# A fused hybrid layer on one core: one scan, one load, the gate's matmuls and one residual are moved in their queues

## The chip, the cores and the metric

The kernel runs on one core of a Trainium2 chip. Its time is the device time of one execution in microseconds (us). The median of three runs of the kernel before is 702.98 us (702.5 to 704.5).

## The reference

One transformer-like layer in float32 for 512 tokens of width 1024:

- The input is normalised and projected to an S5 branch `u` (512 channels) and to q, k, v of 8 heads of 64.
- S5 branch: a diagonal complex state space in 32 groups, then `y = gelu(C s + d_skip * u)` and the gate `y * sigmoid(y @ w_glu + b_glu)`, with `w_glu` 512x512.
- Attention branch: block attention with a relative bias and a softmax per head.
- Both branches are normalised, joined and multiplied with `w_out`, and added to the input.
- Cross attention of 4 heads of 128 over 256 memory rows follows (`x_wq`, `x_wkv`, `x_wo`), and is added.
- A feed-forward block follows: `w_up` (1024 to 5632), a causal convolution of width 3, `silu(gate) * val`, `w_down`, and is added.

## The kernel before

All five engines run programs written out by hand in Bass, one block for each engine, and every engine takes its instructions in the order written. Semaphores link them. Helpers: `filled`/`read` say that TensorE has filled a PSUM bank and that somebody may read it, `drained`/`fill` say that a bank has been read and may be filled again. `plan()` lists for each of the eight banks which result follows which. So a matmul group can wait for the reader of the result that stood in the same bank before.

**Matmuls in three passes.** Each float32 product is taken as hi*hi + hi*lo + lo*hi (`mm3`, L515 to L517). Weights come in "units" of 128x1024 numbers, two to a "chunk" of 1 MB. `load_chunk` (L461 to L468) waits until the two units that stood in its half of the raw buffer have been split, `hi_done` and `lo_done`, and then issues the transfer. For chunk c it waits for 2(c-1) high parts and as many low parts. `split_hi` (ScalarE, L487) makes the high part in a ring of four units, `split_lo` (VectorE, L498) the low part, and TensorE waits for `lo_done`. Some chunks are loaded from SyncE's queue and chunks 4 to 10 from ScalarE's own program, where the wait of `load_chunk` stands in front of all that ScalarE has behind it.

**S5 stages.** The state space goes in four quarters q. For each, TensorE makes `w1r`, `w1i`, the kernels `ka`, `kb` and the states `vr`, `vi`. VectorE's `scan(q)` reads the states in PSUM and writes `zb`. ScalarE copies the kernels into `kt`, and SyncE's `t_load(q)` (L618) spreads them into the Toeplitz matrix `toep` by eight small DMAs. `outputs(q, ...)` on TensorE needs `toep` and the scan. The result goes out and back through DRAM (`y_write`, `y_back`), VectorE adds the skip (`skip_in`), ScalarE takes `gelu(q)`, and GpSimd splits it for the gate (`glu_input`, `glu_in`). Between these TensorE works on the q, k, v and memory projections. After the fifth of eight q/k units, TensorE transposes q in four parts, `qt0` to `qt3`, which go to banks 6, 7, 6, 7, and ScalarE's `qt_evac` empties them. The transposes stand between the four tiles of unit 10.

**The attention loop** has 32 steps s (4 token tiles x 8 heads). TensorE works at even s: in steps 0 to 6 two tiles of the memory's v (`mv_tile`), in the steps of `GLU_AT` the gate's matmuls (`glu_half`, six matmuls of 512 columns each; gate m goes to result `zm`), then the products with v of the step before (`values`), the scores of the next two heads (`scores`), and the transposes of two probability tiles (`pt`). ScalarE takes at odd s the copy of a `pt` and the exponentials of two heads, then what the tables say: `split_hi` of a unit (`SPLIT_AT`), the gate's tanh, `gelu(3)` (an activation table of its own, so that a table is loaded before it and again before the next exponential), `mem_rows("mv", ...)`, which empties `mv0` at s = 7 and `mv1` at s = 9. VectorE takes `logits` of two heads (the bias and the maximum), the copy of a `pt`, `skip_in(3)` at s = 4, the rows of the memory's k at s = 5, and `split_lo` one step behind `split_hi`. The banks say: `mv0` then `z1` in bank 2, `mv1` then `z2` in bank 0, `mk1`, `z0`, `z3` in bank 1.

**Before the feed-forward block** VectorE works in this order: `xo_lo(3)`, `x3_mean(1)`, `x3_rows(1)` (it waits for a power taken on GpSimd), `w_residual(2)` for both halves of 512 columns, `x_lo("x3", 0)`, `split_lo(U_UP)`, `x_lo("x3", 1)`. The last is what the first matmul of `up_half` waits for.

Of the kernel before, what the change touches and what calls it, by code (L numbers as in the profile page):

```python
# [59 lines left out]

GLU_AT = [8, 10, 12, 14]
SS_AT, MK_ROWS_AT = 19, 2

SOUT_AT = [(16, 0, 0), (16, 0, 1), (18, 1, 0), (20, 0, 2), (20, 0, 3), (22, 1, 2), (22, 1, 1), (24, 1, 3), (24, 2, 0),
# [2 lines left out]

XO_AT = [5, 6, 7, 8]  # L70

SPLIT_AT = {0: 22, 1: 23, 2: 24, 4: 25, 9: 26, 11: 27, 13: 28, 16: 29, 29: 30, 31: 31}
YA_AT = [20, 22, 27]


# [25 lines left out]
def layer(nc, A, out):  # L101
# [10 lines left out]
    with ctx:  # L112
# [255 lines left out]
        def after_drain(eng, name, r=0):  # L368

            bank, n = uses[name]  # L370
            eng.wait_ge(bank_free[bank], r + (n + 1))
# [89 lines left out]
        def load_chunk(eng, c, r=0):  # L461
            if c >= 2:

                eng.wait_ge(hi_done, r * 4 + 2 * (c - 1))
                eng.wait_ge(lo_done, r * 4 + 2 * (c - 1))
            src = chunk_src(c, r)
            eng.dma_start(raw[:, c % 2, :].rearrange("p (k n) -> p k n", k=src.shape[1]), src)\
               .then_inc(raw_in[c % 2], 16)  # L468
# [424 lines left out]
        def _(act):  # L893
# [67 lines left out]
            c = COL["attn_qn"]  # L961
# [51 lines left out]
            def kt_evac(t):  # L1013
                c = COL["attn_kn"]
                drained(A_(kT[:, :, t * 128:(t + 1) * 128], read(act, f"kt{t}")[:, :].rearrange("p (a b) -> p a b", a=4),
                           ACT.Copy, scale=gcol[:, c:c + 1]), f"kt{t}")

            def gelu(q):
                act.wait_ge(zz_ready, q + 1)
                A_(to_tokens(yT[:, q, :]), uT[:, q, :].rearrange("p (i k) -> p i k", i=L), ACT.Gelu_apprx_tanh)\  # L1020
                    .then_inc(gelu_ready, 1)
# [48 lines left out]
                kt_evac(t - 1)  # L1070
            split_hi(act, 19)
            kt_evac(TT - 1)
            load_chunk(act, 10)
            split_hi(act, 20)
            for q in range(3):
                gelu(q)
            split_hi(act, 21)

            def mem_rows(name, dst, t):
# [43 lines left out]
            for s in range(TT * H):  # L1123
                if s % 2 == 1:
                    pt_evac(act, lambda o, i: A_(o, i, ACT.Copy), s - 1)
                if s % 2 == 1 and s + 1 < TT * H:
                    probabilities(s + 1)
                    if s > H and s % H == 1:
                        factors_in(s // H - 1)
                    probabilities(s + 2)  # L1130
                if s in GLU_AT:
                    m = GLU_AT.index(s)

                    if m == 0:
                        act.wait_ge(hb_ready, 1)
                    drained(A_(sg[:, m, :], read(act, f"z{m}")[:, :], ACT.Tanh, scale=0.5, bias=hbglu[:, m:m + 1]), f"z{m}")
                if s - 2 in GLU_AT:
                    c = GLU_AT.index(s - 2)
                    act.wait_ge(y2_ready, c + 1)
                    g = COL["gnorm_ssm"] + c  # L1140
                    A_(xs[:, 0, c, :], yT[:, c, :], ACT.Copy, scale=gcol[:, g:g + 1]).then_inc(act_hi, 1)
                    A_(sg[:, c, :], yT[:, c, :], ACT.Square).then_inc(ysq_ready, 1)
                if s in SPLIT_AT:
                    split_hi(act, SPLIT_AT[s])
                if s == 4:
                    gelu(3)
                if s in (7, 9):
                    mem_rows("mv", xv, s // 9)
                if s in YA_AT:
                    ya_square(YA_AT.index(s))  # L1150
                if s - 1 in YA_AT:
                    ya_hi(YA_AT.index(s - 1))
# [122 lines left out]
        def _(dve):  # L1275
# [62 lines left out]
            def head_rows(name, src, tiles, heads, width):  # L1338
                root(name)
                for t in tiles:  # L1340
                    c = EVC[name] + (t - tiles[0]) * heads
                    v = src[:, t, :].rearrange("p (h n) -> p h n", h=heads)
                    tt(v, v, rs[:, c:c + heads].unsqueeze(2).to_broadcast([128, heads, width]), ALU.mult)\
                        .then_inc(xn_ready, 1)
# [172 lines left out]
            head_event("q", qk, range(TT), H, "q")  # L1517
            split_lo(dve, 10)
            head_rows("q", qk, range(TT), H, HD)
            after_drain(dve, "par")  # L1520
            b = COL["ssm_b_glu"]
            V.tensor_scalar_mul(hbglu[:, :], gcol[:, b:b + 4], 0.5).then_inc(hb_ready, 1)
            split_lo(dve, 11)
            root("mem", mem_ready)
            scan(1)
            split_lo(dve, 12)
            split_lo(dve, 13)
            skip_in(0)
            head_event("k", qk, (0, 1), H, "k", False)
# [67 lines left out]
            for s in range(TT * H):  # L1597
                if s % 2 == 1 and s + 1 < TT * H:
                    logits(s + 1)
                    logits(s + 2)  # L1600
                if s % 2 == 1 and s + 1 < TT * H:
                    p = pt_evac(dve, V.tensor_copy, s)
                if s >= H and s % H == 0:
                    inverse_sums(s // H - 1)
                if s == SS_AT:
                    drained(V.tensor_copy(ev(sq, "ss"), p[:, 384:384 + TT]), f"pt{SS_AT}")
                    after_drain(dve, f"pt{SS_AT}")
                    mean_sq("ss")
                    root("ss")
                    dve.wait_ge(h_in, 16 * TT)  # L1610
                if s > H and s % H == 2:
                    ya_scale(s // H - 1)
                if s == 4:
                    skip_in(3)
                if s in (MK_ROWS_AT, MK_ROWS_AT + 1):
                    t = s - MK_ROWS_AT
                    head_event("mk", mkrow, [t], XH, "mk", t == MT - 1)
                if s == MK_ROWS_AT + 3:
                    head_rows("mk", mkrow, range(MT), XH, XD)
                if s - 3 in GLU_AT:  # L1620
                    cc = GLU_AT.index(s - 3)
                    g = gcol[:, COL["gnorm_ssm"] + cc:COL["gnorm_ssm"] + cc + 1]
                    lo_of(yT[:, cc, :], xs[:, 0, cc, :], xs[:, 1, cc, :], g).then_inc(ym_ready, 1)
                if s - 1 in YA_AT:
                    ya_lo(YA_AT.index(s - 1))
                if s - 1 in GLU_AT:
                    m = GLU_AT.index(s - 1)
                    after_drain(dve, f"z{m}")
                    stt(yT[:, m, :], sg[:, m, :], 1.0, yT[:, m, :], ALU.add, ALU.mult).then_inc(y2_ready, 1)
                for n, at in enumerate(G_ADD_AT):  # L1630
                    if at == s:
                        g_residual(n)
                if s - 1 in SPLIT_AT and SPLIT_AT[s - 1] != U_OUT + 3:
                    split_lo(dve, SPLIT_AT[s - 1])
                if s == 2 * H + 2:
                    split_lo(dve, U_OUT + 3)
# [44 lines left out]
            def xo_lo(t):  # L1681
                v = [bs[:, i, :].rearrange("p (a n) -> p a n", a=4)[:, :, t * 128:(t + 1) * 128] for i in range(2)]
                tile_lo(f"xo{t}", v[0], v[1])
# [53 lines left out]
            x3_rows(0)  # L1737
            w_residual(1, [1])
            xo_lo(TT - 1)
            x3_mean(1)  # L1740
            x3_rows(1)
            w_residual(2)
            x_lo("x3", 0)
            dve.wait_ge(lo_done, U_UP)
            split_lo(dve, U_UP)
# [56 lines left out]
        def _(pe):  # L1802
# [383 lines left out]
            for s in range(0, TT * H, 2):  # L2186
                if s < H:
                    mv_tile(s)
                    mv_tile(s + 1)
                if s in GLU_AT:  # L2190
                    for half in range(2):
                        pe.wait_ge(glu_in, 2 + 2 * half)
                        glu_half(GLU_AT.index(s), half)
                for at, t, i in SOUT_AT:
                    if at == s:
                        sout_piece(t, i)
                if s >= 2:
                    values(s - 2)
                if s + 2 < TT * H:
                    scores(s + 2)  # L2200
                prob_transposes("pt", "sc", s, s // H + 1, 4)
                prob_transposes("pt", "sc", s + 1, s // H + 1, 4, s + 1 != SS_AT)
                if s >= H and s % H == 0:
                    factors(s // H - 1)
                if s + 1 == SS_AT:

                    pe.wait_ge(ones_ok, 1)
                    pe.wait_ge(ysum_ready, 1)
                    p = pb[uses[f"pt{SS_AT}"][0]]
                    for t in range(TT):  # L2210
                        last = mm(p[:, 384 + t:385 + t], sg[:, 0, t * 128:(t + 1) * 128], ones[:, 0:1])
                    filled(last, f"pt{SS_AT}")
# [191 lines left out]
```

## Time and profile before

| | |
|---|---|
| median of 3 runs | 702.98 us (702.5 to 704.5) |
| the profiled execution | 705.13 us |
| its span, first to last instruction | 703.5 us |
| TensorE busy | 687.4 us (98%) |
| VectorE, ScalarE, GpSimd busy | 415.0, 320.2, 142.4 us |
| mean granted TensorE clock | 0.998 |

The span is what the trace covers; 1.6 us of the profiled execution's time lie around it. TensorE is busy in all but some 16 us, so the time can only fall where TensorE stands idle, and it rises with every new idle time there. Times in rows are us from the start of the span unless marked ns. PE is TensorE, DVE VectorE, ACT ScalarE, POOL GpSimd, SP SyncE; a q behind the name is the sequencer, which issues DMAs.

### The profile page before, as it was taken

How to read it: one execution, taken by the hardware profiler on the slowest of the kernel's cores; microseconds unless marked ns; L12 is line 12 of the kernel's file. 1: busy time of each engine (PE TensorE's matmuls, PEld its weight loads, DVE VectorE, ACT ScalarE, POOL GpSimd, SP SyncE). 2: the span in 40 equal slices, each digit the busy share in tenths (PEclk: the TensorE clock that was granted, in tenths of full speed). 3: DMA queues.
4: the chain of work that ended last, by engine and by line, in shares of the span. 5: the costliest groups of instructions: out<-in, count | busy, mean ns of one | idle time of the engine just before them, and what ended most of it. 6: DMA issues, size and time to landing. Idle time of an engine off the chain costs nothing.

```text
span 703.5 us, 11258 instructions
## 1 busy us (share of the span) xinstructions
PE 687.4 (98%) x4105; PEld 566.0 (80%) x4105; DVE 415.0 (59%) x697; ACT 320.2 (46%) x559; POOL 142.4 (20%) x139
## 2 busy tenths in 40 slices
PE   8999999988999999999999999999999999999998
PEld 8977767866777788888898888888888888888886
DVE  4999977737765657556865555555455563333333
ACT  5738453656854635664454333333343433222320
POOL 4999994032031111240100000000000000000000
PEclk9999999999999999999999999999999999999999
DMA  8648445258210123030313313223233133132203
GB/s 255 220 136 131 144 106 152 60 184 290 99 61 1 55 96 121 1 119 1 121 62 119 119 60 119 97 82 119 63 116 116 63 119 114 66 119 77 102 0 120
DMA packets 63000, 73.97 MB, mean 105 GB/s; under 512 B 20873, under 2 KB 47796, under 8 KB 62836
## 3 DMA queue, kind: packets, MB, share of 16 engines
q1 hardware_dynamic: 59172, 66.12, 29.8%
q10 hardware_dynamic: 3792, 7.36, 3.2%
q8 instruction: 24, 0.39, 0.3%
q14 instruction: 12, 0.10, 0.0%
HBM read 68.08 MB, written 5.78 MB: 105 GB/s over the span
## 4 chain that ended last, share of the span: by engine, by line
PE 76%; DVE 11%; DMA 4%; ACT 4%; issue 3%; SPq 2%; ACTq 0%; POOL 0%; DVEq 0%
PE pb L515 22%; PE pb L517 22%; PE pb L516 22%; PE pb L1804 6%; DVE F L1286 4%; PE pb L1807 4%; DVE wring L498 2%; ACT F L902 1%; DMA raw<-in_w_in 1%; DMA raw<-in_ssm_w_glu 1%; DMA raw<-in_x_wkv 1%; DMA scr_y<-F 1%; SPq L618 1%; DVE F L1292 1%; DVE pb L1286 1%
## 5 line engine op out<-in xcount | busy, mean ns | idle before, releaser
L515 PE MATMUL pb<-xs,wring 128*128 128x512 f32 (+1 forms) x448 | 165.3, 369 | 1.0 <-DVE xs L1292 1.0
L498 DVE TENSOR_TENSOR wring<-raw,wring 128x1024 fp32r<-128x1024 f32 x95 | 124.1, 1309 | 69.0 <-ACT wring L487 68.8
L517 PE MATMUL pb<-xs,wring 128*128 128x512 f32 (+1 forms) x448 | 164.3, 367 | 0.0
L516 PE MATMUL pb<-xs,wring 128*128 128x512 f32 (+1 forms) x448 | 164.3, 367 | 0.0
L487 ACT ACTIVATE wring<-raw 128x1024 fp32r<-128x1024 f32 x100 | 105.1, 1054 | 89.2 <-PE pb L517 70.1
L1292 DVE SCALAR_TENSOR_TENSOR F<-pb,ccol,F 128x511 f32<-128x511 f32 x88 | 66.0, 750 | 103.4 <-ACT F L902 97.5
L515 PE MATMUL pb<-wring,bs 128*128 128x512 f32 x240 | 96.7, 403 | 0.1
L515 PEld LDWEIGHTS pb<-xs,wring 128*128 128x128 f32 x448 | 84.5, 189 | 15.3 <-issue 1.4
L517 PEld LDWEIGHTS pb<-xs,wring 128*128 128x128 f32 x448 | 84.5, 189 | 13.6
L516 PEld LDWEIGHTS pb<-xs,wring 128*128 128x128 f32 x448 | 84.6, 189 | 13.6
L517 PE MATMUL pb<-wring,bs 128*128 128x512 f32 x240 | 94.1, 392 | 0.0
L516 PE MATMUL pb<-wring,bs 128*128 128x512 f32 x240 | 94.0, 392 | 0.0
L902 ACT ACTIVATE F<-pb,ccol 128x512 f32<-128x512 f32 x44 | 34.2, 778 | 121.4 <-PE pb L517 117.5
L515 PE MATMUL pb<-wring,xs 128*128 128x512 f32 x192 | 81.1, 422 | 0.5 <-DVE wring L501 0.3
L517 PE MATMUL pb<-wring,xs 128*128 128x512 f32 x192 | 75.4, 393 | 0.0
L516 PE MATMUL pb<-wring,xs 128*128 128x512 f32 x192 | 75.1, 391 | 0.0
L1804 PE MATMUL pb<-F 128*64 128x64 f32 (+6 forms) x1056 | 63.3, 261 | 6.9 <-DMA F<-F 2.1
L1804 PEld LDWEIGHTS pb<-F 128*64 128x64 f32 (+4 forms) x1056 | 47.5, 144 | 24.7 <-issue 16.1
L902 ACT ACTIVATE F<-pb 16x128 f32<-16x128 f32 (+5 forms) x84 | 31.1, 383 | 56.0 <-PE pb L1807 44.6
L515 PEld LDWEIGHTS pb<-wring,bs 128*128 128x128 f32 x240 | 45.4, 189 | 9.9 <-POOL wring L869 0.3
L517 PEld LDWEIGHTS pb<-wring,bs 128*128 128x128 f32 x240 | 45.4, 189 | 9.7
L516 PEld LDWEIGHTS pb<-wring,bs 128*128 128x128 f32 x240 | 45.5, 189 | 8.8
(147 smaller groups left out, 790.3 us busy)
## 6 DMA issues: line engine op xcount, KB each, us to landing
raw<-in_ffn_w_up SPq DMA_DIRECT2D x22, 1024.0 KB, 5.1
raw<-in_ffn_w_down SPq DMA_DIRECT2D x11, 1024.0 KB, 4.8
F<-in_x SPq DMA_DIRECT2D x8, 512.0 KB, 5.9
raw<-in_w_in ACTq DMA_DIRECT2D x4, 1024.0 KB, 5.6
raw<-in_w_out SPq DMA_DIRECT2D x4, 1024.0 KB, 4.8
raw<-in_w_in SPq DMA_DIRECT2D x3, 1024.0 KB, 6.3
raw<-in_x_wkv ACTq DMA_DIRECT2D x3, 1024.0 KB, 6.0
raw<-in_x_wq SPq DMA_DIRECT2D x2, 1024.0 KB, 5.4
```

Source lines behind the costliest of these rows:

```text
L487: ins = nc.scalar.activation(w_unit(u, 0), raw_unit(u), ACT.Copy)
L498: ins = nc.vector.tensor_tensor(w_unit(u, 1), raw_unit(u), w_unit(u, 0).bitcast(f32), ALU.subtract)
L515: nc.tensor.matmul(ps, lh, rh, start=first, stop=False)
L516: nc.tensor.matmul(ps, lh, rl_, start=False, stop=False)
L517: return nc.tensor.matmul(ps, ll, rh, start=False, stop=last)
L618: sync.dma_start(toep[d * CG:(d + 1) * CG, :, (L - 1 - d) * CG:], kt[0:CG, :, 0:(d + 1) * CG]).then_inc(t_in[q], 16)
L902: return nc.scalar.activation(o, i, f, **k)
L1286: return V.tensor_tensor(o, a, b, op)
L1292: return V.scalar_tensor_tensor(out=o, in0=a, scalar=s1, in1=b, op0=o1, op1=o2)
L1804: return nc.tensor.matmul(o, l, r, start=start, stop=stop)
L1807: return nc.tensor.transpose(o, i, ident[0:i.shape[0], 0:i.shape[0]])
```

## The change

The change moves work in the queues and adds or removes none:

1. VectorE: `scan(1)` comes straight after the q rows, ahead of `split_lo(11)`, the gate's bias, `split_lo(12)` and the memory's root.
2. ScalarE: `gelu(0)` and `gelu(1)` stand ahead of `load_chunk(act, 10)` and `split_hi(act, 20)`; `gelu(2)` stays behind them.
3. Attention loop: the gate's four tiles no longer take two halves each at s = 8, 10, 12, 14. The first halves of gates 0 and 1 stand at s = 8, their second halves at s = 10. The tanh of the four is at s = 10, 11, 12, 14, and what follows it on ScalarE and VectorE moves with it.
4. `split_hi(24)` moves from s = 2 to s = 3 (and its `split_lo` from 3 to 4), `gelu(3)` from s = 4 to s = 5, where it stands behind the exponentials of that step.
5. VectorE: `w_residual(2)` is cut: the first half goes ahead of `x3_mean(1)`, the second ahead of `x3_rows(1)`.

```
-GLU_AT = [8, 10, 12, 14]
+GLU_AT = {8: [(0, 0), (1, 0)], 10: [(0, 1), (1, 1)], 12: [(2, 0), (2, 1)], 14: [(3, 0), (3, 1)]}
+TANH_AT = [10, 11, 12, 14]
-SPLIT_AT = {0: 22, 1: 23, 2: 24, 4: 25, 9: 26, 11: 27, 13: 28, 16: 29, 29: 30, 31: 31}
+SPLIT_AT = {0: 22, 1: 23, 3: 24, 4: 25, 9: 26, 11: 27, 13: 28, 16: 29, 29: 30, 31: 31}
@@ ScalarE
             kt_evac(TT - 1)
+            gelu(0)
+            gelu(1)
             load_chunk(act, 10)
             split_hi(act, 20)
-            for q in range(3):
-                gelu(q)
+            gelu(2)
             split_hi(act, 21)
...
-                if s in GLU_AT:
-                    m = GLU_AT.index(s)
+                if s in TANH_AT:
+                    m = TANH_AT.index(s)
...
-                if s - 2 in GLU_AT:
-                    c = GLU_AT.index(s - 2)
+                if s - 2 in TANH_AT:
+                    c = TANH_AT.index(s - 2)
...
-                if s == 4:
+                if s == 5:
                     gelu(3)
@@ VectorE
             head_rows("q", qk, range(TT), H, HD)
+            scan(1)
+            split_lo(dve, 11)
             after_drain(dve, "par")
             b = COL["ssm_b_glu"]
             V.tensor_scalar_mul(hbglu[:, :], gcol[:, b:b + 4], 0.5).then_inc(hb_ready, 1)
-            split_lo(dve, 11)
+            split_lo(dve, 12)
             root("mem", mem_ready)
-            scan(1)
-            split_lo(dve, 12)
             split_lo(dve, 13)
...
-                if s - 3 in GLU_AT:
-                    cc = GLU_AT.index(s - 3)
+                if s - 3 in TANH_AT:
+                    cc = TANH_AT.index(s - 3)
...
-                if s - 1 in GLU_AT:
-                    m = GLU_AT.index(s - 1)
+                if s - 1 in TANH_AT:
+                    m = TANH_AT.index(s - 1)
...
             xo_lo(TT - 1)
+            w_residual(2, [0])
             x3_mean(1)
+            w_residual(2, [1])
             x3_rows(1)
-            w_residual(2)
             x_lo("x3", 0)
@@ TensorE
-                if s in GLU_AT:
-                    for half in range(2):
-                        pe.wait_ge(glu_in, 2 + 2 * half)
-                        glu_half(GLU_AT.index(s), half)
+                for m, half in GLU_AT.get(s, []):
+                    pe.wait_ge(glu_in, 2 + 2 * half)
+                    glu_half(m, half)
```

## Rows read from the trace of the kernel before

**Rows 1.** Waits of TensorE: engine, tile, line <- releaser: total us, times, longest.
```profile
PE pb L1804 <- ACT pbuf L902: 2.1, 2, 1.7
...
PE pb L1804 <- ACT F L902: 0.7, 1, 0.7
```

**Rows 2.** Timeline of TensorE, 81 to 92: start, duration, what, [idle before <- releaser].
```profile
85.06 0.60 PE L1807 MATMUL pb<-ident,F 128*128 128x128 f32 x4
...
90.38 0.84 PE L1804 MATMUL pb<-F 128*64 128x64 f32 x24 [1.51 <-DVE F L1286]
```

**Rows 3.** Timeline of VectorE, 77 to 91.
```profile
77.04 1.55 DVE L1286 TENSOR_TENSOR F<-F,rs 128x512 f32<-128x512 f32 x1
...
79.46 1.22 DVE L498 TENSOR_TENSOR wring<-raw,wring 128x1024 fp32r<-128x1024 f32 x1
...
84.14 0.42 DVE L1286 TENSOR_TENSOR pb<-pb,F 128x256 f32<-128x256 f32 x1
...
90.09 1.68 DVE L498 TENSOR_TENSOR wring<-raw,wring 128x1024 fp32r<-128x1024 f32 x1
```

**Rows 4.** Timeline of ScalarE and its sequencer, 76 to 89.
```profile
80.76 0.37 ACTq L467 DMA_DIRECT2D raw<-in_w_in  x1
82.09 0.69 ACT L902 ACTIVATE F<-pb,gq 128x512 f32<-128x512 f32 x1 [4.19 <-PE pb L1807]
```

**Rows 5.** Timeline of GpSimd, 75 to 92.
```profile
84.28 1.42 POOL L810 TENSOR_TENSOR F<-F 128x576 f32<-128x576 f32 x1
```

**Rows 6.** Timeline of ScalarE, 103.5 to 107, around the load of chunk 8.
```profile
104.84 0.38 ACTq L467 DMA_DIRECT2D raw<-in_x_wkv  x1
105.05 0.83 ACT L902 ACTIVATE F<-pb 16x128 f32<-16x128 f32 x3
```

**Rows 7.** Timeline of ScalarE, 135.8 to 145, around the load of chunk 10.
```profile
137.02 0.69 ACT L902 ACTIVATE F<-pb,gcol 128x512 f32<-128x512 f32 x1
137.08 0.39 ACTq L467 DMA_DIRECT2D raw<-in_x_wkv  x1
143.43 1.06 ACT L487 ACTIVATE wring<-raw 128x1024 fp32r<-128x1024 f32 x1 [5.72 <-DMA raw<-in_x_wkv]
```

**Rows 8.** Timeline of SyncE, 131 to 159: the eight DMAs of `t_load(3)`.
```profile
131.92 6.18 SPq L618 DMA_DIRECT2D F<-F  x8
```

**Rows 9.** Timeline of TensorE at four later places.
```profile
143.63 1.11 PE L1804 MATMUL pb<-F 128*64 128x64 f32 x24 [2.12 <-DMA F<-F]
...
171.99 0.71 PE L1804 MATMUL pb<-F 64*128 64x128 f32 x8 [1.73 <-ACT pbuf L902]
...
172.83 0.48 PE L515 MATMUL pb<-xs,wring 128*128 128x512 f32 x1
...
337.89 0.36 PE L515 MATMUL pb<-xs,wring 128*128 128x256 f32 x1 [1.00 <-DVE xs L1292]
```

**Rows 10.** Windows: stretch: us, busy by engine, then granted clock, DMA share, GB/s.
```profile
143.90:147.30 3.40, 3.40 (x29) 2.38 (x24) 0.00 (x0) 3.37 (x4) 0.22 (x1) 0.50 0.21 48
...
170.30:172.00 1.70, 0.01 (x2) 0.04 (x2) 1.12 (x1) 1.53 (x5) 1.62 (x2) 1.00 0.74 277
```

**Rows 11.** Timeline of ScalarE, 163 to 175.
```profile
164.19 1.06 ACT L487 ACTIVATE wring<-raw 128x1024 fp32r<-128x1024 f32 x1 [3.22 <-DMA raw<-in_ssm_w_glu]
...
167.08 1.28 ACT L902 ACT_TABLE_LOAD   x1
168.37 1.25 ACT L902 ACTIVATE F<-F 128x512 f32<-128x512 f32 x1
...
174.23 0.69 ACT L902 ACTIVATE F<-pb,rs 128x512 f32<-128x512 f32 x1
```

**Rows 12.** Timeline of VectorE, 163 to 174.
```profile
167.13 0.28 DVE L1590 CUSTOM_DVE_ANT_0 pb<-pb,F 128x128 f32<-128x128 f32 x1
...
169.79 1.63 DVE L498 TENSOR_TENSOR wring<-raw,wring 128x1024 fp32r<-128x1024 f32 x1
```

**Rows 13.** Timeline of VectorE, 331 to 338.
```profile
332.71 1.28 DVE L1292 SCALAR_TENSOR_TENSOR F<-pb,F 128x512 f32<-128x512 f32 x2
```

## The prediction

> **What bounds the kernel now.** I read the page first: TensorE is busy 98% of the span, so an edit is worth only what it does to TensorE's idle places. Then the waits of TensorE, longest first, and the timeline at each. Four places matter. At 90.38 it waits 1.51 for the second scan [rows 2]. At 143.63 it waits 2.12 for the Toeplitz DMAs of the last quarter [rows 9]. Between 165 and 172 it waits for ScalarE three times: 0.7 for the copy of a probability tile, 2.1 in two waits for exponentials, the longest 1.73, 2.8 in all [rows 1, 9]. At 337.89 it waits 1.00 for VectorE [rows 9]. If all of it went, 1.5 + 2.1 + 2.8 + 1.0 = 7.4 us would be gained. The question is what is late next at each place.
>
> **Part 1, the scan sooner.** The q rows end at 77.04 + 1.55 = 78.6; the scan takes 84.14 to 90.09, 6.0 us [rows 3]. Placed at 78.6 it ends at 84.6, ahead of the 88.9 at which TensorE wants it, and the 1.51 goes. But `split_lo(11)`, which ended at 79.46 + 1.22 = 80.7, now starts only behind the scan. `load_chunk(7)` waits for exactly this split: its DMA goes out at 80.76, 0.1 behind it [rows 3, 4]. That load stands in ScalarE's program ahead of `qt_evac(0)`, which ran at 82.09 [rows 4]. TensorE needs it: `qt2` goes into the bank of `qt0` and is due at 85.06 [rows 2]. New chain: at 84.6 a GpSimd operation is running, 84.28 to 85.70 in the old trace [rows 5]; without the split in between I put its end at 84.85. Then 1.2 split, to 86.05; issue of the load at 86.1, 0.4 long; copy of 0.7, to 87.25; `qt2` at 87.3 instead of 85.06. So 1.5 goes and 2.25 comes: +0.7. Bounds: no wait for GpSimd, +0.4; one whole GpSimd operation of 1.4 more than nothing, +1.9. `qt3` finds its bank: the high part and copy behind add 1.75 to 87.25, and `qt3` is due at 87.3 + 1.8. The other moved operations (bias, root, `split_lo(12)`) keep the queue's sum; unit 12 is wanted only after 99. What depends on TensorE up to 154 shifts with it.
>
> The Trainium skill (SBUF — State Buffer, "SBUF: two separate sides") says that a VectorE operation with two SBUF inputs and a GpSimd operation lock each other out for a whole instruction. By it the split waits for GpSimd's boundary; without it the part gives +0.4.
>
> **Part 2, the load of chunk 10 later.** The eight small DMAs are issued from 131.92 to 138.10 [rows 8]. The chunk's load goes out at 137.08, before the last of them, and lands by 143.43; TensorE is released at 143.63 [rows 7, 9]: the last small DMA seems to queue behind the megabyte. Were the load issued behind 138.1, the wait would go. It isn't, I think. ScalarE's sequencer runs ahead of its engine: at 104.84 it issued a load that stands behind three copies which had not started (105.05, x3) [rows 6]. Here it would have to pass a table load and two gelus, also three, whose inputs are long there. So the DMA goes out some 0.1 after 137.08, still ahead of the last small one at about 137.5. I take 0. Bounds: nothing, and the whole 2.1 gained. Nothing is lost: the gelus then run in ScalarE's 5.72 us of idle [rows 7], and a load later by two gelus still feeds a unit wanted ten us on.
>
> The Trainium skill (Advanced Engine Details and Errata, "Engine Queue Depths") gives ScalarE a queue of 8 instructions on trn2. By it, as by the trace, three pass, and the part gives 0.
>
> **Parts 3 and 4, the attention loop.** Before, `split_hi(24)` at s = 2 held ScalarE until its chunk landed at 164.19 [rows 11], and behind it stood the copy and the exponentials of s = 3; then the gelu of s = 4 with its two table loads, 1.28 + 1.25 + 1.28 [rows 11], held those of s = 5. Both move behind their exponentials, so all three waits (2.8) go and TensorE would be at the gate at 172.83 - 2.75 = 170.1. There it does `z0`'s first half, six matmuls or 1.4 us, and at 171.5 wants bank 2 for `z1`. That bank holds `mv0`, emptied by `mem_rows` at s = 7, now behind the gelu, a table load and the exponentials of that step. VectorE: `logits` of s = 5 stay at 167.13 (the skip and the split ahead of them only swap); the copy, the root and the rows follow as before, and `split_lo(25)`, at 169.79 [rows 12], takes 1.2 as in [rows 3] instead of 1.63, to 171.0; then `logits(8)`, 0.5, to 171.5. ScalarE: exponentials of s = 5 to 168.4, table 169.7, gelu to 170.95, copy to 171.1, wait to 171.55, table to 172.8, two exponentials 1.0 to 173.8, `mem_rows` 0.69 [rows 11] to 174.5. `z1` starts at 174.55. Before, the sixth to twelfth gate matmuls of this step started at 172.83 + 1.4 = 174.2. So this part gives +0.35: 2.8 of stalls become one of 3.0. Bounds: -2.8, if the bank is free in time; +0.8, if the split meets GpSimd for 0.4 more. Behind it the tanh, the splits and the sums have steps of slack, and ScalarE stops for no tanh at s = 8; 0.
>
> **Part 5, the residual cut.** The first half fits where VectorE waits for the square (the mean comes 0.3 later, and so the row), the second where it waits for GpSimd's power. Of the 1.28 for both halves [rows 13] between the row and `x_lo`, 1.2 go and 0.3 comes back: 0.9 of the 1.00 [rows 9] goes. Bounds -1.0 and -0.3 (if the later row holds the transposes of the second tile, due right behind it). **-0.9.**
>
> **The clock.** Behind the 2.12 stall the granted clock was 0.50 (1.2 GHz) from 143.9 to 147.3; behind the 1.73 stall it stayed at 1.00 [rows 9, 10]. A fall of 3.4 us at half rate costs up to 1.7. At 143 it cost little, for what ends the stalls at 165 to 172 is ScalarE and a DMA. The new stall of 3.0 is longer than the one that lost the clock, and at most 1.7 follows; part of the slow stretch may lie in the stall itself: I take 1.2.
>
> **Sum:** +0.7 + 0 + 0.35 - 0.9 + 1.2 = +1.35. The profiled execution would go from 705.13 to 706.5; it lies 2.15 over the median of 702.98, and I carry the difference over: 704.3.
>
> **Rivals.**
> - Clock and lock, slower: the stall at `qt2` (2.2 us) loses the clock as well, for its full 1.7, and the split meets a whole GpSimd operation (half of part 1's upper bound of +1.2, as an average): 704.3 + 1.7 + 0.6 = 706.6. The place is 87 to 92; it decides from a stall there of about the 2.12 that lost the clock before. For it: all up to 154 hangs on TensorE, nothing takes it back. Against: 1.51 and 1.73 didn't lose it.
> - One of the two new stalls is not there. Without that at `qt2`: -1.5 + 0.35 - 0.9 + 1.2 = -0.85, or 702.1. Without that at `z1`, and so no fall there: 0.7 - 2.8 - 0.9 = -3.0, or 700.0. Against both: the order in the programs is plain.
> - The load does go out behind the last small DMA: 2.1 less, 702.2. For it: only 0.4 us part the two.
> - All works as its shape suggests: -1.5 - 2.1 - 2.8 - 0.9 = -7.3, or 695.7.
> - The page would not change but for `x_lo`: VectorE and ScalarE serve the same waits elsewhere, each part near 0: 702 to 703.
>
> **Chances.** Forecast 0.42 (702.9 to 705.3 by itself: with no fall of the clock, with its full 1.7), slower rival 0.23, one new stall missing 0.15, load behind 0.06, all works 0.08, no change 0.06. Within 0.3%, about what a measurement of this kernel can tell from no change, is 700.9 to 705.1. Slower than that: the rival, and the upper end of the forecast, 0.28. Faster: all works, the case without the stall at `z1`, some of the load, 0.18. Same 0.54. For eight in ten the range is 700.0 to 706.6.
>
> **What would show it.** Right: TensorE idle some 2.2 before `qt2`, none at the second scan; the chunk's load within 0.3 of its old place against the last small DMA and the 2.1 still there; no waits for exponentials at 165 to 172, but one of 3 us for ScalarE before a gate matmul; the wait before the feed-forward block 0.1 to 0.3; half clock behind a new stall. Wrong: no idle time at `qt2` (ScalarE's load doesn't hold its copies), the load issued after 138, or `mv0` emptied before TensorE asks.

## The result, and the profile after

| | before | after |
|---|---|---|
| median | 704.71 us (702.5 to 705.97, 8 runs) | 707.5 us (705.14 to 708.79, 8 runs) |
| ratio | | 1.0042 [1.0024, 1.0061] |
| profiled execution, its span | 705.13, 703.5 us | 706.97, 705.4 us |

The changed kernel is slower by 0.42%, some 3.0 us (2.8 between the two medians). The forecast was +1.35 us and 704.3, and its range ended at 706.6, so the time lies outside. Of the 3.2 us between 704.3 and 707.5, 1.7 belong to the kernel before: the forecast was set upon the 702.98 of three executions, and eight gave 704.71. A second set of 12 runs (below) gave 1.0054.

The waits of TensorE after, by line and releaser (total us, times, longest):

```profile
PE pb L516 <- ACT F L903: 3.5, 1, 3.5
PE pb L1810 <- ACT F L903: 3.4, 4, 2.1
...
PE pb L1807 <- ACT pbuf L903: 1.9, 1, 1.9
```

The same waits in the timeline of TensorE after:

```profile
87.71 0.63 PE L1810 MATMUL pb<-ident,F 128*128 128x128 f32 x4 [2.07 <-ACT F L903]
...
157.08 0.49 PE L1807 MATMUL pb<-F 64*128 64x128 f32 x4 [1.87 <-ACT pbuf L903]
...
171.40 0.40 PE L518 MATMUL pb<-xs,wring 128*128 128x512 f32 x1
175.33 0.47 PE L516 MATMUL pb<-xs,wring 128*128 128x512 f32 x1 [3.53 <-ACT F L903]
```

Every wait of [rows 2] and [rows 9] is gone: the second scan's 1.51, the Toeplitz 2.12, the 1.73 for exponentials and the 1.00 ahead of the feed-forward block. In their place stand three: 2.07 at `qt2`, 1.87 at the first exponentials, 3.53 at `z1`. Two of them were forecast, at 2.2 and 3.0. Their chains, first that at `qt2`: VectorE, ScalarE and GpSimd after.

```profile
83.25 0.76 DVE L1288 TENSOR_TENSOR F<-pb,F 128x256 f32<-128x256 f32 x2
83.92 2.40 DVE L499 TENSOR_TENSOR wring<-raw,wring 128x1024 fp32r<-128x1024 f32 x1
```

```profile
86.41 0.37 ACTq L468 DMA_DIRECT2D raw<-in_w_in  x1
86.88 0.69 ACT L903 ACTIVATE F<-pb,gq 128x512 f32<-128x512 f32 x1 [8.57 <-DVE wring L499]
```

```profile
83.81 1.42 POOL L811 TENSOR_TENSOR F<-F 128x576 f32<-128x576 f32 x1
85.31 4.21 POOL L698 TENSOR_TENSOR F<-F,pw 128x576 f32<-128x576 f32 x2
```

The scan ends at 84.0 and `split_lo(11)` starts there, but lasts 2.40 instead of 1.22: the GpSimd operation that runs since 83.81 ends at 85.23, and 1.1 us later so does the split. The load goes out at 86.41, behind it the copy of `qt0`, and at 87.6 `qt2` has its bank. (This agrees with the exclusive lock of the Trainium skill, SBUF — State Buffer, "SBUF: two separate sides".)

At `z1`, ScalarE after:

```profile
169.19 1.28 ACT L903 ACT_TABLE_LOAD   x1
170.48 1.28 ACT L903 ACTIVATE F<-F 128x512 f32<-128x512 f32 x1
171.52 0.34 ACT L903 ACTIVATE F<-pb 128x128 f32<-128x128 f32 x1
172.29 1.28 ACT L903 ACT_TABLE_LOAD   x1 [0.42 <-DVE nmx L1592]
...
174.50 0.69 ACT L903 ACTIVATE F<-pb,rs 128x512 f32<-128x512 f32 x1
```

The last row is `mem_rows("mv", ...)`. TensorE asked for its bank at 171.80 (the first half of `z0` had just ended) and went on at 175.33.

Then the clock. Windows after (us, busy by engine, granted clock, DMA share, GB/s), the stretch of the wait and the one behind it:

```profile
171.60:175.30 3.70, 0.20 (x1) 0.00 (x1) 1.22 (x7) 3.15 (x8) 2.43 (x3) 1.00 1.05 390
...
175.90:179.30 3.40, 3.40 (x17) 2.15 (x15) 0.00 (x0) 0.00 (x0) 0.00 (x0) 0.50 0.15 61
```

TensorE was busy for 0.20 of 3.70 us, and behind that the clock was granted at 0.50 (1.2 GHz) for 3.4 us. In the second trace of the changed kernel the clock fell twice, at 158.3 behind the wait for exponentials and at 175.4, at the end of that at `z1`.

A single trace doesn't say how often that happens. The mean granted clock of every timed execution does: (1 - mean clock) x span is the time lost to the lower level. It is 1.24 us on average in 97 executions of the kernel before, and 4.24 us in the 8 of the changed kernel (4.59 in the 12 taken again). One fall of 3.4 us loses 1.7, so this would be 0.7 falls an execution before and 2.5 to 2.7 after, an estimate from these means.

A lost microsecond need not be a microsecond of time. Within each kernel, one execution against the others, 1 us more lost goes with 0.62 us more time (95%: 0.50 to 0.75, 248 executions in all), and with 0.93 (0.66 to 1.20) in the 20 of the changed kernel. This is a relation between executions and not an experiment.

### The profile page after: what moved, and what is told of

It reads as the page before. It is cut to its first block, busy times and chain, and to the rows that moved or that the text cites. A ratio compares the mean times of both kernels' runs of the same rounds, so it can differ in the third digit from the quotient of the medians.

```text
span 705.4 us, 11258 instructions
## 1 busy us (share of the span) xinstructions
PE 688.3 (98%) x4105; PEld 565.9 (80%) x4105; DVE 413.6 (59%) x697; ACT 320.2 (45%) x559; POOL 139.7 (20%) x139
## 4 chain that ended last, share of the span: by engine, by line
PE 87%; ACT 3%; DMA 3%; DVE 3%; SPq 2%; issue 2%; ACTq 0%; DVEq 0%
PE pb L516 25%; PE pb L518 25%; PE pb L517 24%; PE pb L1807 8%; PE pb L1810 5%; ACT F L903 2%; SPq L632 1%; DMA scr_y<-F 1%; DMA raw<-in_x_wkv 1%; DVE wring L499 1%; DVE F L1288 1%; SPq L619 1%; ACT xs L903 1%; DMA F<-scr_b 0%; DMA F<-scr_y 0%
```

## The experiments

Each ran beside the kernel before on its chip; ratios are to that. "Lost" is the loss just defined, averaged over the kernel's executions (before: 1.24 us).

| kernel | median us (runs) | ratio [95%] | lost us |
|---|---|---|---|
| part 1 alone | 707.73 (11) | 1.0034 [1.0022, 1.0046] | 1.73 |
| part 1 with the split first | 704.11 (12) | 0.9978 [0.9966, 0.9989] | 1.46 |
| parts 3 and 4 alone | 707.10 (12) | 1.0020 [1.0005, 1.0036] | 2.23 |
| the same, `mv0` emptied earlier | 702.96 (6) | 0.9961 [0.9948, 0.9975] | 0.82 |
| part 2 alone | 705.47 (12) | 1.0007 [0.9990, 1.0024] | 1.76 |
| part 5 alone | 703.95 (12) | 0.9985 [0.9969, 1.0002] | 1.23 |
| after, both stalls mended | 701.40 (6) | 0.9942 [0.9925, 0.9959] | 2.10 |
| before, load 10 waits | 703.52 (12) | 0.9974 [0.9957, 0.9991] | 1.35 |
| after, TensorE kept at work ahead of `z1` | 707.01 (12) | 1.0038 [1.0021, 1.0056] | 2.59 |
| after, mended, load 10 waits | 698.13 (6) | 0.9913 [0.9887, 0.9938] | 0.23 |
| after again | 707.63 (12) | 1.0054 [1.0034, 1.0073] | 4.59 |
| part 1, load 10 waits | 705.35 (12) | 1.0000 [0.9986, 1.0014] | 2.29 |
| before, load 10 waits, again | 702.70 (6) | 0.9959 [0.9943, 0.9975] | 1.40 |
| after, load 10 waits | 705.88 (12) | 1.0008 [0.9994, 1.0021] | 4.23 |

**Part 1 alone.** The kernel before with the change's order of VectorE around `scan(1)`.

> The kernel before with part 1 alone: the second scan ahead of split_lo(11). Theory (the split holds the load of chunk 7, and the load holds ScalarE's copy of qt0): TensorE idles 2.1 us before the third q transpose, none at the second scan, and reaches the second quarter's outputs 0.7 us later than before (1.1 in the raw times of the changed kernel, of which 0.4 is a later start); no other part is needed for it; the time is 0 to 2 us over the kernel before. Rival (the stall at the third transpose comes from something else that the change moves): idle time there under 0.5 us and the time 1 us or more under the kernel before.

TensorE waited 2.13 at `qt2` and not for the scan, and its later matmuls stood 0.7 later (at 90 us and at 128 us; 0.9 at the end), as forecast. But the kernel is 0.34% slower, 2.4 us, not 0.7. The clock stayed whole behind this stall; the wait and a window of this kernel:

```profile
87.82 0.63 PE L1807 MATMUL pb<-ident,F 128*128 128x128 f32 x4 [2.13 <-ACT F L902]
```

```profile
87.90:91.30 3.40, 3.40 (x20) 2.85 (x20) 3.30 (x6) 2.57 (x4) 3.24 (x3) 1.00 0.96 329
```

**Part 1 with the split first.** It tells whether the scan's place or the split's costs. Against part 1 alone:

```
             head_rows("q", qk, range(TT), H, HD)
+            split_lo(dve, 11)
             scan(1)
-            split_lo(dve, 11)
```

> As the run with part 1 alone, but split_lo(11) stays ahead of the scan; bias, split_lo(12) and root stay behind it. Theory: the load goes out as early as before, no stall at the third transpose, and the scan, ending about 1.5 us before it is needed, leaves no stall either: TensorE is 1.5 us earlier at the second quarter's outputs. Of these 1.5 us little reaches the end if the bias rows bound the first softmax (the rival to 'TensorE's time adds up'): then the wait before the first probability transposes grows by about as much, and the time gains under 0.5 us; if it adds up, 1.5 us.

No wait at `qt2` and none for the scan, and 0.22% faster than before. So the 2 us at `qt2` are the split's, or rather the load's that waits for it and stands ahead of the copy. Its one trace, of the slowest of its 12 executions, gives all of the 1.5 back later (waits of 1.24 for the last Toeplitz DMA, 1.81 for the first exponentials, 1.71 and 1.72 around the first gate, and a fall of the clock behind the last); the timed runs keep 1.6.

**Parts 3 and 4 alone**, the attention loop's edits.

> The kernel before with parts 3 and 4 alone (gate halves, split 24, gelu 3, tanh). Theory (bank of the memory's first v tile, emptied behind a gelu and two table loads): the waits at 165 to 172 are gone or under 0.5 us together, one wait of 3.0 to 3.6 us stands in the middle of the step's gate matmuls, released by ScalarE, and at the end of that step TensorE is within 1 us of the kernel before, plus up to 1.7 us where the clock falls behind the stall; time +1 to +3 us. Rival (the loss in the changed kernel comes from the earlier parts): time 1 us or more below the kernel before.

```profile
174.53 0.47 PE L516 MATMUL pb<-xs,wring 128*128 128x512 f32 x1 [3.53 <-ACT F L903]
```

That is the same wait at `z1` as in the whole change, in a kernel in which nothing else is changed. The cost is 0.20%, 1.4 us; the forecast's +0.35 for the queues and 1.2 for the clock make 1.55. The lost time rose by 1.0.

**The same, with `mv0` emptied earlier.**

```
-                if s in (7, 9):
+                if s in (6, 9):
```

> As the run with parts 3 and 4 alone, with one more move: ScalarE empties the memory's first v tile at s = 6, right behind the gelu, instead of at s = 7 behind a table load and two exponentials. Theory (the bank is what stalls): the 3 to 3.6 us stall shrinks to under 1 us, the exponentials come 0.6 us later, and TensorE is 2 to 3 us earlier behind the step than with parts 3 and 4 alone; the clock no longer falls there; time 1 to 4 us below that run. Rival (ScalarE's work between the exponentials, not the bank, is the bound): the stall only moves to the scores of the same step and the time stays within 0.7 us of that run.

ScalarE and TensorE of this kernel:

```profile
171.04 1.28 ACT L903 ACTIVATE F<-F 128x512 f32<-128x512 f32 x1
172.09 0.67 ACT L903 ACTIVATE F<-pb,rs 128x512 f32<-128x512 f32 x1
...
172.93 1.28 ACT L903 ACT_TABLE_LOAD   x1
```

```profile
172.90 0.47 PE L516 MATMUL pb<-xs,wring 128*128 128x512 f32 x1 [0.54 <-ACT F L903]
...
175.39 0.72 PE L1805 MATMUL pb<-F 64*128 64x128 f32 x8 [0.51 <-ACT pbuf L903]
```

One number in one line turns 0.20% slower into 0.39% faster: the copy now stands between the gelu and the table load, the wait of 3.53 is one of 0.54, and the lost time is 0.82 instead of 2.23. The two medians are 4.1 us apart; 3.0 less of stall and 1.4 less lost to the clock make 4.4.

**Part 2 alone**, two gelus ahead of the load of chunk 10.

> The kernel before with part 2 alone (two gelus written ahead of the load of chunk 10). Theory: the load's DMA goes out within 0.2 us of its old place behind the last copy of k, since the sequencer passes a table load and two gelus; whether the last small Toeplitz DMA is issued before it is decided by SyncE's own issue times, not by this move; time within 0.7 us of the kernel before. Rival (the move orders the two): the load goes out 3 us later and the 2.1 us wait for the Toeplitz DMAs is gone because of it.

No difference that can be measured, as forecast. ScalarE in the whole change shows why:

```profile
138.19 0.69 ACT L903 ACTIVATE F<-pb,gcol 128x512 f32<-128x512 f32 x1
138.25 0.42 ACTq L468 DMA_DIRECT2D raw<-in_x_wkv  x1
138.89 1.28 ACT L903 ACT_TABLE_LOAD   x1
140.19 2.17 ACT L903 ACTIVATE F<-F 128x512 f32<-128x512 f32 x2
```

The load is issued 0.06 behind the start of the copy, the very distance of [rows 7], though a table load and two gelus now stand ahead of it in the program. But here, in part 2 alone and in the whole change, the wait for the last Toeplitz DMA was absent. SyncE's row after says what had moved:

```profile
133.09 5.11 SPq L619 DMA_DIRECT2D F<-F  x8
138.25 0.58 SPq L624 DMA_DIRECT2D scr_y<-F  x1
```

The eight small DMAs took 5.11 us to issue, 6.18 in [rows 8]; so the last was out when the megabyte was issued. Durations of the eight issues (ns, least/median/longest) and their time to landing, before and then after:

```profile
L618 SPq DMA_DIRECT2D F<-F x8: 601/603/1655, 131.9 to 137.5; - x8
...
DMA to landing us min/median/max: 1.8/2.4/6.1
```

```profile
L619 SPq DMA_DIRECT2D F<-F x8: 599/600/612, 133.1 to 137.6; - x8
...
DMA to landing us min/median/max: 1.9/2.1/2.5
```

Part 5 alone leaves this stretch untouched, and its trace has 5.12 and no wait either. Of the eleven traces in which the load isn't held back, five have one issue of 1.1 to 1.7 us instead of 0.6, always ahead of the load; these five have the wait (0.72 to 2.71), and the other six have none. The 2.12 of the trace before stands only in some executions, and it was read as fixed.

**Part 5 alone**, the residual cut.

> The kernel before with part 5 alone. Theory: the wait before the first feed-forward matmul falls from 1.0 to 0.1 us, nothing else changes, TensorE is 0.9 us earlier from there to the end; time 0.9 us less. Rival (the later row holds the transposes of the second tile): 0.3 us or less.

The wait ahead of the feed-forward block is gone in its trace, and from 281 us to the end TensorE won 0.9; 0.15% is 1.1 us. The interval touches no change.

**After, both stalls mended**: the split first, and `mv0` at s = 6.

> The changed kernel with two moves more: split_lo(11) ahead of the second scan, and the memory's first v tile emptied at s = 6. Theory (the two new waits are the whole loss, and the clock falls behind them): no stall at the third q transpose, under 1 us in the gate's step, TensorE at the feed-forward block 4 to 7 us earlier than in the changed kernel; time 699 to 702 where the kernel before has 704.7, so 3 to 6 us less, faster than both. Rival (the time is lost in the clock's falls whatever the stalls): not more than 1 us below the kernel before.

0.58% faster than before. TensorE did not wait at `qt2`, and 0.53 at the gate. In this trace the Toeplitz wait was back, and the clock fell behind it:

```profile
143.38 0.84 PE L1807 MATMUL pb<-F 128*64 128x64 f32 x24 [2.71 <-DMA F<-F]
```

```profile
144.90:148.30 3.40, 3.40 (x30) 2.25 (x30) 0.00 (x0) 0.00 (x0) 0.00 (x0) 0.50 0.33 75
```

**Before, load 10 waits**, so that the megabyte can't be issued ahead of a small DMA.

```
+            act.wait_ge(t_in[3], 16 * L)
             load_chunk(act, 10)
```

> The kernel before with one wait more: ScalarE issues the load of chunk 10 only when all small Toeplitz DMAs of the last quarter have landed. Theory (the last small DMA queues behind the megabyte when it is issued after it): TensorE's 2.1 us wait shrinks to under 0.5 us, the clock does not fall there, and TensorE is some 3.5 us earlier at 150; but the bias rows come only as early as the DMAs before them let them, so that a wait of 1 to 3 us appears before the first probability transposes, and the time changes by less than 1.5 us. Rival (TensorE's time adds up): 2 us or more less.

No Toeplitz wait, and the wait of 1 to 3 us that I expected before the first probability transposes did not come either. It gives 0.26%, and 0.41% when taken again. S5's result also came back from DRAM sooner: `y_back` was issued from 138.60 instead of 144.15, and at 157 us TensorE was 5.1 us ahead of the trace before (each counted from its own lead or lag at 80 us), of which 3.1 were left at the end. 1.6 of that lead has another source, told below.

**After, with TensorE kept at work ahead of `z1`**: 12 matmuls more, whose result is overwritten, ahead of the first half of `z0`. The stall is filled and not shortened.

```
+                if m == 0 and half == 0:
+                    for _ in range(12):
+                        mm(p[:, :], w_unit(u, 0)[:, 0, at], xs[:, 0, 4, :])
```

> The changed kernel with twelve idle-filling matmuls of 512 columns (2.7 us) into z0's bank ahead of z0's first half; their result is overwritten, so the output is unchanged. They take the place of most of the 3.5 us stall before z1 and shorten nothing. Theory (the changed kernel loses its time largely to the granted clock, which falls behind the stalls): the wait before z1 shrinks to 0.8 us at the same place, the clock no longer falls behind it, TensorE is 1.5 to 1.8 us earlier behind the step, fewer falls per execution, and the time is 1 to 2 us below the changed kernel although more work is done. Rival (only the stall itself costs): the same time within 0.5 us, or slower.

Its TensorE, and its window behind the place:

```profile
171.22 3.02 PE L1807 MATMUL pb<-xs,wring 128*128 128x512 f32 x12
...
175.94 0.47 PE L516 MATMUL pb<-xs,wring 128*128 128x512 f32 x1 [0.35 <-ACT F L903]
```

```profile
175.90:179.30 3.40, 3.23 (x22) 2.19 (x22) 0.68 (x3) 0.24 (x1) 0.00 (x0) 1.00 0.49 198
```

`z1` starts 0.6 later than in the trace after, and yet the lost time falls from 4.59 to 2.59 (to 4.24 in the first set: 1.65 less), and the clock was whole behind the place. So the fall at this place belongs to the idle time; the trace has another, at 158.5, behind the 1.83 at the first exponentials. The time itself went from a median of 707.63 to 707.01, and from a mean of 708.15 to 706.96, both with 12 runs on one chip and intervals that overlap: 2.0 of clock less 0.6 of work would have left 1.4, so what a fall costs in time this run leaves open.

**After again.** The changed kernel itself, beside the one just told.

> The changed kernel itself once more, for its falls of the clock and as the neighbour of the two others. Theory: at least one fall in nearly every execution, mostly behind the gate's stall, a mean clock of 0.992 to 0.997, and 2 to 4 us above the kernel before. Rival (the three falls of four of its executions were the chip's mood): as few falls as the kernel before and less than 2 us above it.

1.0054, in line with 1.0042. Its two falls stand behind a wait of 2.30 (at 157.43) and at the end of one of 2.31 (at `z1`). The second wait is shorter than 3.53 since TensorE, slowed from 158.3 on, asked for the bank 1.4 later.

**After, mended, and load 10 waits**: the three edits together.

> The changed kernel with the two mended places and the load of chunk 10 held until the small Toeplitz DMAs have landed. Theory (the three places are independent up to the bias rows): no wait for the Toeplitz DMAs, none above 1.2 us from 60 to 210, TensorE another 1 to 3 us earlier at 160 than with the two mended places alone; time 0.5 to 3 us below that kernel, the fastest of all. Rival (the gelus written before the load, which now waits, or the later chunk 10 hold the first softmax): the time is that of the two mended places within 0.5 us or above it.

0.87% faster than before, the fastest of all; its whole gate, TensorE:

```profile
167.14 0.47 PE L516 MATMUL pb<-xs,wring 128*128 128x512 f32 x1 [0.55 <-ACT F L903]
169.63 0.71 PE L1808 MATMUL pb<-F 64*128 64x128 f32 x8 [0.51 <-ACT pbuf L903]
171.34 0.63 PE L1811 MATMUL pb<-ident,F 128*128 128x128 f32 x4 [0.41 <-ACT F L903]
```

No wait over 0.6 us is left between the first transposes and 330 us, and the clock lost 0.23 us on average of six executions.

**Where does part 1's cost come from?** Two more, with the meeting of megabyte and small DMA taken out of both.

> Part 1 (the scan sooner) in the kernel before, with the load of chunk 10 held until the last Toeplitz DMA has landed. To be read against e13_waits_again, which is the same without part 1. If the extra cost of part 1 comes from the last small DMA meeting the megabyte load, e12 is 0.7 us slower than e13, the delay at qt2 less the scan's wait, and no more. If it comes from the chain behind (S5 result through DRAM, bias, first exponentials), the delay grows there as well and e12 is 1.3 to 2.4 us slower.

> The kernel of e8_load_waits again, on this chip: 703.5 us, ratio 0.997 to before, no wait of TensorE at the last Toeplitz matrix.

Part 1 costs 705.35 - 702.70 = 2.65 us (ratios 1.0000 and 0.9959, intervals apart), so it isn't that meeting. The lost time differs by 0.9, which leaves 1.75 where 0.7 was forecast. A lead is in the two traces of the kernel without part 1: the scan's wait is not in every execution of the old order. VectorE's rows in its first trace, then in its second, and TensorE's in the second:

```profile
72.84 5.32 DVE L1287 TENSOR_TENSOR F<-F,rs 128x512 f32<-128x512 f32 x4
...
82.57 0.16 DVE L1287 TENSOR_TENSOR rs<-rs,rt 128x2 f32<-128x2 f32 x1
```

```profile
73.04 6.24 DVE L1287 TENSOR_TENSOR F<-F,rs 128x512 f32<-128x512 f32 x4
...
83.81 1.08 DVE L1287 TENSOR_TENSOR rs<-rs,rt 128x2 f32<-128x2 f32 x1
```

```profile
91.06 0.84 PE L1805 MATMUL pb<-F 128*64 128x64 f32 x24 [1.40 <-DVE F L1287]
```

In the first, the root was done at 82.73, in the second at 84.89, of which 0.3 is a later start; and in the first TensorE did not wait for the scan at all. Starts of the same matmul against the trace before, each counted from its difference at 80 us (us):

| | at 90 us | at 158 us | at the end |
|---|---|---|---|
| load 10 waits, first trace | -1.6 | -5.1 | -3.1 |
| load 10 waits, second trace | -0.1 | -3.6 | -1.3 |
| the same with part 1 | +0.4 | -3.3 | -1.1 |

So part 1 costs 0.5 (at 90 us) and 0.2 (at the end) against the second trace, 2.0 and 2.0 against the first. Six of seven traces with the old order have the wait, at 1.16 to 1.51.

**After, load 10 waits.** The two stalls stay, and only the load is held.

> The changed kernel with only the load of chunk 10 held until the last Toeplitz DMA has landed; the stalls at qt2 (2.1) and z1 stay. e10_best has both mended and the same wait, 698.1. If the two stalls cost their length and a fall each, this is 698.1 + 2.1 + 0.6 + 3.0 + 1.3 = 705. If z1's stall is bounded by ScalarE's order behind the exponentials, it stays 3 us or more though TensorE's work before it comes 4 us sooner, and the time is again 705 to 706; if the earlier exponentials carry the gelu with them, the stall shrinks and it is 702 to 703.

```profile
172.27 0.77 PE L516 MATMUL pb<-xs,wring 128*128 128x512 f32 x1 [3.53 <-ACT F L903]
```

The stall at `z1` is 3.53 again, though TensorE stood at the gate 3 us sooner: it isn't TensorE that is early, ScalarE's order behind the exponentials sets it, and it moves along with them. Against the mended kernel with the same wait (698.13) the two stalls cost 7.8 us by the medians, which are of two chips, and 6.7 by the ratios: 2.0 and 3.5 of idle time against 0 and 0.55, which is 5.0, and 4.0 more lost to the clock, of which some lies inside the stall at `z1` (here the clock fell at 171.1, 1.2 us before its end).

## Why the prediction was wrong

The two stalls were forecast at their places and nearly at their sizes. The step that failed is the clock's term, 1.2 for a loss that rose by 3.0 to 3.4, and beside it the term of part 1, +0.7 for a measured +2.4. A third is in no term of the sum: the base of 702.98, which was 1.7 too low, so that 704.3 would have been 706.1 with the same +1.35.

- **Part 1, "+0.7".** At the place: right. 1.51 went, 2.07 to 2.13 came (forecast 2.25), and in the trace of part 1 alone TensorE stood 0.7 later up to 140 us, 0.9 at the end. In time: +2.4 [+1.6, +3.2]. 0.5 of the excess is clock (1.73 against 1.24 lost). The rest, 1.2, is open. Where the scan's wait is missing in an execution of the old order, part 1 has nothing to win and costs its whole 2; were that so in most timed executions, it would be the rest. Against this stands that part 1 with the split first, whose trace shows only this wait removed, did win 0.22%. A trace shows only profiled executions, so no run here tells how often it is missing in timed ones. The meeting of megabyte and small DMA is ruled out.
- **Part 2, "0".** Right: +0.07%, and the load at its old distance. The reason given was right as well. What the forecast missed is that the 2.12 beside it was no fixed stall: it depends on whether one of SyncE's issues takes half a microsecond to a whole one longer, so "the 2.1 still there" failed in the trace after, without the change having removed it. Nor was it worth its length: TensorE met 1.87 at the first exponentials instead.
- **Parts 3 and 4, "+0.35".** Right in kind: the three waits of 2.8 became one at `z1`. It was 3.53 for 3.0; in the trace after TensorE asked 0.3 later than forecast (171.8 for 171.5) and the bank came 0.8 later (175.3 for 174.55), all of it there already at the first table load (169.19 for 168.4). With the clock, +1.4 measured against 1.55.
- **Part 5, "-0.9".** Right: -0.95 in the trace, -1.1 in time [-2.2, +0.1].
- **The clock, "I take 1.2": the term that was mis-sized.** The loss rose by 3.0 us in the first set and 3.4 in the second. Three things were wrong. It was reckoned from the profiled execution as if that had one fall and every other too; the executions before had 0.7. And only the longest stall was charged, when the waits of about 2 us at the exponentials, which take the place of the Toeplitz wait, lose the clock as well in some executions (at 158 in two of three traces that have it in the change's order). And that a wait of 1.73 keeps the clock was read from one trace, from a window that shows the wait and not what follows it [rows 10]; the last section has what other traces show. With 3.0 to 3.4 in place of 1.2, the forecast's own sum is +3.15 to +3.55; measured were +3.0 and +3.8. That this agreement is not partly luck isn't shown. At 0.62 to 0.93 us of time for 1 us lost, the clock's share is 1.9 to 3.2 and not the whole 3.0 to 3.4, which leaves room for part 1's open 1.2. And by the parts alone the clock's loss rises by 2.0 (0.5 + 0.5 + 1.0), not by 3.0. How much of the miss is clock and how much part 1 stays open.
- **Two small sums** of the prediction don't close: with no fall and with a whole one its forecast runs from 703.1 to 704.8, not 702.9 to 705.3, and part 1's two bounds lie 1.5 apart for one GpSimd operation of 1.4. Neither moves the +1.35.

The slower rival came nearest (706.6), on the same low base and by a wrong mechanism: it let the clock fall behind `qt2`. In six traces with that stall the clock fell there in none. What it got right is that the split meets a whole GpSimd operation.

The four parts by themselves add up: 2.4 + 0.5 + 1.4 - 1.1 = +3.2.

## What to carry to other kernels

When a TensorE-bound kernel trades several short waits for one long one of equal sum, it may not be neutral: the short ones lose the clock in some executions, the long one did in every trace (1.24 us lost on average before, 2.23 with parts 3 and 4 alone). Count what is lost to the clock from the mean granted clock of all executions, not from one trace, and treat a wait that depends on two DMAs issued 0.4 us apart as a chance, not as a row. When an operation is moved ahead on one engine, look at what it was moved past: here both stalls came from a short item (a split that a load waits for, a copy that frees a bank) left behind a longer one, and putting the short one first turned +0.42% into -0.58%.

## What the runs showed of the hardware

- The same idle time doesn't always lose the clock. Seven traces have a wait of 1.72 or 1.73 at the first gate. Behind it the clock stayed at 1.00 in the trace before and in that of part 1 alone, and fell to 0.50 within 1.7 us in the five others (part 1 with the split first, part 2 alone, load held twice, part 1 with the load held). A window of the first, then one of the last:

```profile
172.00:175.40 3.40, 3.40 (x21) 2.86 (x22) 1.13 (x6) 1.85 (x6) 1.16 (x2) 1.00 1.02 376
```

```profile
170.00:173.40 3.40, 3.40 (x15) 2.77 (x15) 1.16 (x6) 1.77 (x6) 0.98 (x2) 0.51 1.00 367
```

  With part 5 alone it fell 1.6 us behind a wait of 1.36. Behind 1.82 to 2.13 at `qt2` it never fell in six traces; at 3.53 at `z1` it fell in all three that have it, in two behind the wait and in one inside it.
- A small DMA (at most 64 KB) whose issue isn't over when a megabyte is issued on another queue lands late. In the trace before it was issued from 137.50, 0.4 behind the megabyte, and landed at 143.58, the megabyte at 143.41 [rows 7 to 9]. In all five such traces it took 5.2 to 6.9 us, in the other eleven 2.4 to 2.5. With the load held behind the small ones no trace shows a wait of TensorE for it, and 0.26 to 0.41% came back.
- The run of one VectorE program beside GpSimd has more than one course: four q rows took 5.32 us in one execution and 6.24 in another of the same kernel (GpSimd's two operations beside them took 3.08 and 2.54, the other way round), and single traces of it end 2.1 us apart.
